# Three edits to a one-core decoder layer: matmuls of 512 columns in the second FFN's out stages, the eighth early weight slab loaded last, a_proj's merged parts made later

## The reference, cut to what matters

```python
h = modulate(x, norm_ffn1, sh1, sc1)
x = x + 0.5 * g1 * swiglu(h, w_ffn1_in, w_ffn1_out)     # (silu(h @ Wa) * (h @ Wb)) @ W_out
h = modulate(x, norm_mix, sh2, sc2); proj = h @ w_in     # z, xBC, dt, u, gates
p_a = ssd_mixer(...) @ w_a_proj                          # "a_proj"
p_b = glu_a * sigmoid(glu_g)                             # from the S5 branch
merged = sigmoid(gate_a) * p_a + sigmoid(gate_b) * p_b
x = x + g2 * (merged @ w_out)
h = modulate(x, norm_ffn2, sh3, sc3)
x = x + 0.5 * g3 * swiglu(h, w_ffn2_in, w_ffn2_out)     # D_FF = 5504
return rms_norm(x, norm_final)
# mods (sh1 ... g3) = silu(c) @ w_ada + b_ada, nine vectors of 2048
```

## Time and profile before

| | before |
|---|---|
| three timed runs | 2510.43, 2515.06, 2516.42 us, median 2515.06 |
| the profiled execution | 2511.76 us, of which its span is 2510.0 |
| PE busy | 2411.1 us, 96% of the span |
| VectorE (DVE), ScalarE (ACT) busy | 1730.3 us (69%), 1037.4 us (41%) |
| mean granted TensorE clock | 0.988 of full |
| HBM read and written | 232 GB/s over the span |

### The profile page before, as it was taken

How to read it: one execution, slowest core, us unless ns; L and a number is a source line. 1 busy time by engine, 2 the same in 40 slices (tenths; PEclk the granted TensorE clock), 3 DMA queues, 4 the chain that set the end, 5 groups by cost and what they waited for, 6 DMA issues and landing times.

```text
span 2510.0 us, 39646 instructions
## 1 busy us (share of the span) xinstructions
PE 2411.1 (96%) x16260; PEld 2187.6 (87%) x16260; DVE 1730.3 (69%) x2028; ACT 1037.4 (41%) x1111; POOL 227.8 (9%) x257
## 2 busy tenths in 40 slices
PE   6799999999999999999999999999999999999998
PEld 3488799888899999889899999999888899888998
DVE  3376877778778778888976776776877455444543
ACT  3243343443443454444345444333433444344433
POOL 1421313142223000000000000000000000000000
PEclk8999999999999999999999999999999999999999
DMA  9986877878787865555565466787678556555652
GB/s 359 382 267 242 295 263 259 292 252 308 259 279 267 305 235 169 180 175 198 177 228 167 142 212 221 254 299 250 234 273 297 168 184 202 188 192 172 197 177 97
DMA packets 296997, 584.69 MB, mean 233 GB/s; under 512 B 10324, under 2 KB 35412, under 8 KB 295316
## 3 DMA queue, kind: packets, MB, share of 16 engines
q1 hardware_dynamic: 291408, 559.98, 65.3%
q0 software_dynamic: 4144, 22.28, 2.5%
q10 hardware_dynamic: 1300, 0.35, 0.1%
HBM read 569.98 MB, written 12.58 MB: 232 GB/s over the span
## 4 chain that ended last, share of the span: by engine, by line
PE 49%; DVE 6%; ACT 1%; issue 1%; ACTq 0%; DVEq 0%
PE gps L305 45%; PE mps L305 3%; DVE wlo L914 2%; DVE t L1441 1%; DVE acc L932 1%; ACT whi L537 1%; PE mps L1721 0%; DVE tab L1484 0%; DVE wi L1478 0%; DVE E L1403 0%; DVE wi L1456 0%; DVE wr L1452 0%; DVE wr L1474 0%; DVE xw L1129 0%; DVE E L1408 0%
## 5 line engine op out<-in xcount | busy, mean ns | idle before, releaser
L914 DVE TENSOR_TENSOR wlo<-raw,whi 128x1024 fp32r<-128x1024 f32 x800 | 986.5, 1275 | 584.9 <-ACT whi L537 582.1
L537 ACT ACTIVATE whi<-raw 128x1024 fp32r<-128x1024 f32 x800 | 803.2, 1052 | 1239.3 <-PE gps L305 1204.1
L305 PE MATMUL gps<-whi,hs 128*128 128x512 f32 (+1 forms) x2816 | 875.3, 388 | 16.6 <-DVE wlo L914 11.8
L305 PEld LDWEIGHTS gps<-whi,hs 128*128 128x128 f32 x2816 | 528.9, 188 | 141.5 <-issue 22.3
L305 PE MATMUL gps<-hs,whi 128*128 128x256 f32 x3072 | 566.8, 287 | 16.8 <-DVE wlo L914 12.1
L305 PE MATMUL gps<-wlo,hs 128*128 128x512 f32 (+1 forms) x1408 | 542.9, 386 | 0.0
L305 PEld LDWEIGHTS gps<-hs,whi 128*128 128x128 f32 x3072 | 483.7, 194 | 27.3 <-DVE wlo L914 15.0
L305 PE MATMUL gps<-ffs,whi 128*128 128x256 f32 x2752 | 498.7, 284 | 5.3 <-DVE wlo L914 5.3
L305 PE MATMUL gps<-hs,wlo 128*128 128x256 f32 x1536 | 437.1, 285 | 0.0
L305 PEld LDWEIGHTS gps<-ffs,whi 128*128 128x128 f32 x2752 | 429.1, 192 | 7.2 <-DVE wlo L914 6.9
L305 PE MATMUL gps<-ffs,wlo 128*128 128x256 f32 x1376 | 389.3, 283 | 0.0
(11 more groups left out here) (270 smaller groups left out, 1412.9 us busy)
## 6 DMA issues: line engine op xcount, KB each, us to landing
raw<-in_w_ffn_in_dram SPq DMA_DIRECT2D x160, 1024.0 KB
raw<-in_w_ada_dram SPq DMA_DIRECT2D x112, 1024.0 KB
raw<-in_w_in_dram SPq DMA_DIRECT2D x80, 1024.0 KB
raw<-in_w_ffn_out_dram SPq DMA_DIRECT2D x56, 1024.0 KB
pre<-in_w_ada_dram SPq DMA_DIRECT2D x32, 1024.0 KB, 14.3
raw<-in_w_ffn_out_dram SPq DMA_DIRECT2D x40, 768.0 KB
raw<-in_w_b_glu_dram SPq DMA_DIRECT2D x32, 512.0 KB
raw<-in_w_a_proj_dram SPq DMA_DIRECT2D x16, 1024.0 KB
```

The costliest lines, as they stand in the source:

```text
L305: return pe.matmul(out, lhsT, rhs, start=start, stop=stop, skip_group_check=True)
L537: act.activation(whi[:, mpos % SPLIT, h, :], raw[:, pos % RING, h, :], ACT.Copy).then_inc(hi_ready, 1)
L914: ins = dve.tensor_tensor(wlo[:, mpos % SPLIT, h, :], raw[:, pos % RING, h, :], whi[:, mpos % SPLIT, h, :].bitcast(F32), ALU.subtract)
```

## The change

**1. Wide out stages.** In both out stages of the second FFN (`ph.wide`), the high weight block meets both parts of the activation in one matmul of 512 columns, so each product is two matmuls, of 512 and 256 columns. The sums of a tile now stand in two halves of a whole bank (`wps[:, j]`), so a group takes all four banks of `gps`. ACT copies them to SBUF: tiles 0 and 1 when they are complete, tile 2, then tile 3 (`kept`). DVE adds both halves of each kept tile to xT, 8 instructions a group. In the very last group DVE adds straight from PSUM (`add_last`).

**2. The eighth early slab.** Slab m = 7 is loaded behind chunk 7's four blocks. PE does early tiles 18 and 19 after `total(6)` instead of behind chunk 7's first two blocks, tiles 20 and 21 behind the first two, and nothing behind the last two.

**3. a_proj's merged parts.** `merged_hi` goes behind the next slab's `hi` on ACT, `merged_lo` behind the second next slab's `lo` on DVE.

```diff
+        self.wide = evac == "resid" and gate == 2
+        self.rounds = (2 if self.wide else 1) * bodies
...
-                        for m in {0: (), 6: (5, 6, 7), 7: ()}.get(q, (q - 1,)):
+                        for m in {0: (), 6: (5, 6), 7: (7,)}.get(q, (q - 1,)):
...
+                    elif ph.wide:
+                        n = 2 * i + g
+                        if r.t + n:
+                            act.wait_ge(sem("x_added"), r.t + n)
+                        act.wait_ge(sem("tiles_done"), 2 * (r.t + n) + 1)
+                        act.activation(kept[0][:, :, :], wps[:, 0:2, :], ACT.Copy).then_inc(psum_free(0), 1)
+                        act.wait_ge(sem("tiles_done"), 2 * (r.t + n) + 2)
+                        act.activation(kept[1][:, 0, :], wps[:, 2, :], ACT.Copy)
+                        act.wait_ge(slab_done, m_end)
+                        act.activation(kept[1][:, 1, :], wps[:, 3, :], ACT.Copy).then_inc(psum_free(1), 1)
...
-                    act.wait_ge(sem("merged"), n + 1)
-                    act.activation(hs[:, 4 * n:4 * n + 4, 0, :], ga[:, 4 * n:4 * n + 4, :], ACT.Copy
-                                   ).then_inc(sem("merged_hi"), 1)
+
+                    def merged_hi():
+                        act.wait_ge(sem("merged"), n + 1)
+                        act.activation(hs[:, 4 * n:4 * n + 4, 0, :], ga[:, 4 * n:4 * n + 4, :], ACT.Copy
+                                       ).then_inc(sem("merged_hi"), 1)
+
+                    later.append(merged_hi)
...
+                                if later:
+                                    later.pop()()
...
+            def add_kept(ph, n, h):
+
+                dve.wait_ge(psum_free(h), r.q + n + 1)
+                for part in range(2):
+                    for j in range(2):
+                        ins = gated_add(ph, 4 * n + 2 * h + j, kept[h][:, j, S * part:S * part + S])
+                    if part == 0:
+                        link(ins)
+                if h:
+                    ins.then_inc(sem("x_added"), 1)
+                    if ph.norm == 3:
+                        dve.wait_ge(sem("x_added"), r.t + n + 1)
+                        gains(ph, n)
+
+            def add_last(ph, m_end):
+
+                for j in range(4):
+                    if j == 0:
+                        dve.wait_ge(sem("tiles_done"), 2 * (r.t + 3) + 1)
+                    elif j == 2:
+                        dve.wait_ge(sem("tiles_done"), 2 * (r.t + 3) + 2)
+                    elif j == 3:
+                        dve.wait_ge(slab_done, m_end)
+                    link(gated_add(ph, 12 + j, wps[:, j, 0:S]))
+                    gated_add(ph, 12 + j, wps[:, j, S:2 * S]).then_inc(sem("x_new") if j < 3 else psum_free(1), 1)
...
-                    later.append(merged_lo)
+                    later.append(lambda: later.append(merged_lo))
...
+                        if q == 7:
+                            e = (20, 21, -1, -1)[t]
                         if e >= 0:
                             early_tile(e)
                     total(q)
+                    if q == 6:
+                        early_tile(18)
+                        early_tile(19)
...
+                def slab_wide(g, i, s, mp, k0):
+                    for j in range(4):
+                        if s == 0 and j % 2 == 0:
+                            pe.wait_ge(psum_free(j // 2), r.q + 2 * i + g)
+                        for k in range(ph.chunks[s]):
+                            hi = whi[:, mp % SPLIT, k, P * j:P * j + P]
+                            lo = wlo[:, mp % SPLIT, k, P * j:P * j + P]
+                            both = moving[:, k0 + k, :, :].rearrange("p w s -> p (w s)")
+                            mm(pe, wps[:, j, :], hi, both, k0 + k == 0, False)
+                            ins = mm(pe, wps[:, j, 0:S], lo, moving[:, k0 + k, 0, :], False,
+                                     k0 + k == sum(ph.chunks) - 1)
+                        yield ins
```

More of the change, by code:

```diff
@@ L221, in build @@
         gated = at("gated", T, [P, 2, COLS])
+        kept = [half, at("kept1", W, [P, 2, COLS])]
         sq = at("sq", T, [P, 4, S])
@@ L582, in first_two @@
                 for s in range(2):
+                    if s == 1 and between is not None:
+                        between()
                     if i is None:
@@ L678, in gemm @@
                     act.wait_ge(sem("bbar_ready"), 1)
+                if ph.evac == "pair" and r.t:
+                    act.wait_ge(sem("x_added"), r.t)
                 def body(i, nxt):
@@ L691, in body @@
                                 next(side, None)
+                        between = None
+                        if ph.wide:
+                            between = lambda: evacuate(ph, i, 1, m0 + i * mper + 2 * ph.slabs, 0)
                         if g == 0:
@@ L698, in body @@
                         elif nxt == "loop":
-                            first_two(ph, i, side)
+                            first_two(ph, i, side, between)
                         elif nxt is not None and ph.norm is not None:
@@ L702, in body @@
                         elif nxt is not None:
-                            first_two(nxt, side=side)
+                            first_two(nxt, side=side, between=between)
                         if g == 1:
@@ L707, in body @@
                                     pass
-                        evacuate(ph, i, g, m0 + i * mper + (g + 1) * ph.slabs, r.q + i + 1)
-                if ph.bodies > 1 and not ph.side and ph.norm is None and ph.evac != "mul_a":
+                        if not ph.wide or ph.norm is not None and 2 * i + g == 3:
+                            evacuate(ph, i, g, m0 + i * mper + (g + 1) * ph.slabs, r.q + i + 1)
+                if ph.bodies > 1 and not ph.side and ph.norm is None and ph.evac != "mul_a" and not ph.wide:
                     if after_norm:
@@ L965, in first_two @@
                     if s == 1 and between is not None:
-                        multiply(*between)
+                        between()
                     if i is None:
@@ L1091, in body @@
                                 next(side, None)
+                                if ph.wide and gg == 1 and s == 1:
+                                    add_kept(ph, 2 * i, 1)
                         if g == 1:
-                            between = (ph, m0 + i * mper + 2 * ph.slabs, r.q + i + 1) if ph.evac == "pair" else None
+                            m_end, between = m0 + i * mper + 2 * ph.slabs, None
+                            if ph.evac == "pair":
+                                between = lambda: multiply(ph, m_end, r.q + i + 1)
+                            elif ph.wide:
+                                between = lambda: add_kept(ph, 2 * i + g, 0)
                             if nxt == "loop":
@@ L1246, in early @@
             def early(ph, following):
-                first_two(following, between=(ph, 8, 1))
+                first_two(following, between=lambda: multiply(ph, 8, 1))
                 evacuate(ph, 0, 1, 8, 1)
```

68 lines of the change are left out of this document (48 added, 20 removed).

## The result

| | before | after |
|---|---|---|
| median of the timed runs on the same chip | 2515.1 us | 2496.9 us (2492.9 to 2497.5) |
| ratio to before | | 0.993, 95% interval 0.9915 to 0.9946 |
| the profiled execution | 2511.8 us, span 2510.0 | 2496.3 us, span 2494.6 |

The change takes 18 us off; the interval of the ratio leaves out 1. The forecast was 2493, the range 2482 to 2505.

The account below looks back on a forecast made before the run. PE was taken as the bound, busy 96% of the span; terms -9.2 + 0.1 + 0.8 - 4.4 - 7.5 = -20.2 us gave 2491.6 from the profiled execution or 2494.9 from the median, forecast 2493, range 2482 to 2505.

Parts of the forecast that it names:

- 1a: Wide out stages: one matmul fewer in each of 688 products saves 0.0133 us each, 9.2 us off; bounds 0 to 18.3.
- 1b: Group ends of the wide out stages: ACT's copies free the banks 0.86 us before PE wants them, cost 0.
- ACT rival: PE waits for ACT's first copy at seven group starts, 3.75 us each, 26 in all: 2519 us; chance 4%.
- 1c: Tail of the last out stage: last addition ends 1.85 us behind PE against 1.08 before, 0.8 us more.
- 2, the eighth slab: Prologue: chunk 7's first block lands at 111.4, PE starts slab 6 at 125.0 instead of 129.4, 4.4 us off; bounds 0 to 4.9.
- 3, a_proj: Gaps behind a_proj's groups 0 and 2 close, 2 x 3.75 = 7.5 us off, 5.5 at the least, 7.6 at most.
- no slack at all: a_proj: DVE's next `lo` ends at 1597.4, just when PE wants it; perhaps 0.1 to 0.3 us.

Follow-up runs that it names:

- part 2 alone: Kernel before with only the eighth slab loaded last and its early tiles moved: 2509.9 us, ratio 0.9982.
- the low part left in its place: Changed kernel, but in a_proj only the merged high part is made later, the low part as before the change: 2498.0 us, ratio 0.9937.
- the run with one at every group: Changed kernel with throwaway matmuls of 128 to 512 columns (one, or twelve at group 0) at each group's start in the wide out stages: 2498.3 us.
- the last run: Changed kernel plus last group's tile 0 told when complete, wide form in w_out, one 128-column throwaway matmul ahead of first stage's second group: 2492.1 us, ratio 0.9927.
- ACT's copies later: Changed kernel with ACT's copies of a finished group put behind the rounding of the second next slab: 2527.7 us, ratio 1.0059.
- part 1 alone: Kernel before with only the wide out stages, the two other edits undone: 2508.0 us, ratio 0.997.
- grouped by width: Changed kernel with each tile's 512-column matmuls of a slab first, then its 256-column ones, in the wide out stages: 2497.3 us, ratio 0.9938.
- the second run of the changed kernel: The changed kernel measured once more, nothing altered: 2498.0 us, ratio 0.9928.
- part 3 alone: Kernel before with only the edits to a_proj's merged_hi and merged_lo: 2507.5 us, ratio 0.997.

## Why the prediction was right, and where it was not

**1a, the fixed part: right for the second stage, half for the first.** 368 products at 0.3467 give 368 x 0.0133 = 4.9 us, as worked out (4.8 by the stage's length). The 320 of the first took 0.3533, so 320 x 0.0067 = 2.1 where 4.3 was taken. The mis-sized term is 688 x 0.0133 = 9.2; it was 7.0. The step behind it, that two widths agree on 0.0133 and so a mixed pair has the sum of both, was an inference from streams of one width, and the prediction said that no row had a mixed pair. Its bounds (0 to 18.3) held. The Trainium skill (page "TensorE: Matmul & The Clock Gate", section "Back-to-back issue gap") gives N / 2.4 + 2.5 ns for a single warm matmul, by which the pair would take an estimated 325 ns. The traces show 347 and 353, and it does not agree here either.

**1b, evacuation: right.** PE waits for none of the seven copies, with 0.79 to 0.89 us to spare where 0.86 was worked out. The ACT rival stands with its price corrected: seven gaps of 3.1 us, and a half clock behind three.

**1c, the tail: right,** 1.86 us behind PE against 1.85.

**2, the eighth slab: right in its mechanism, and 5.1 us in this execution where 4.4 was worked out and 4.9 was the bound.** Chunk 7's first block at 110.97 (111.4 forecast), the last at 118.99 (119.5), the bias at 121.86 (122.5), slab 6 at 124.55 (125.0), 5.06 us earlier than before. Each step came about half a microsecond earlier than worked out, since the first block did. The kernel with part 2 alone has 4.5 by its ratio. What the working did not see is the idle time that the new order leaves to PE at chunk 7's end, 1.6 us ahead of the last block and 0.7 ahead of the sum. In four of the eleven traces with part 2 the clock fell behind it, and 1.4 to 3 of the 5 us were lost again (last section).

**3, a_proj: right.** 3.7 us at both groups, 7.4 in all (7.5). DVE's chain ran as worked out, its `lo` ending when the slab ahead was done, but "no slack at all" left out the sum of `w_ada` products that PE makes in between; 0.75 us of slack were there. The run with the low part left in its place showed what happens when 1.1 us more stands in that chain, gaps of 0.42.

**The sum.** With what was measured for each, -7.0 + 0.8 - 4.9 - 7.4 = -18.5 us; the medians differ by 18.2. Against the sum of the prediction, -20.2, the 2.2 us of 1a are missing, and part 2 makes up 0.5. The forecast of 2493 was 3.9 too low; about 2 of this is the first stage, and the rest the base, which was set half-way between the profiled execution and the median of the timed ones, where the medians alone gave 2494.9. The profiled executions show only 15.4 us on their spans: the one of the kernel before lay 3.3 us under its median, and the one of the kernel after holds 3.3 us of delays that six others with the same code at that place don't have (below).

## What to carry to other kernels

Price an edit by the start-to-start spacing of the very sequence that it makes; where the trace has only streams of one width, keep a bound on both sides, for a mixed stream can sit at more than one pace. A gap in PE costs its idle time for sure and the half clock behind it only sometimes, so a rival's price has two ends. Start to count a stage's gain ahead of its first wait: 1.4 us in w_out were 0.3 when the wait at its entry was counted too. And when one engine's queue holds a late operation ahead of an urgent one (ACT's rounding ahead of the next slab's `hi`), the order in that one queue is worth most of the gain, here 4.9 of 7.4 us.

## What the runs showed of the hardware

**Two paces of one instruction pair.** A 512-column and a 256-column matmul in turn, at a granted clock of 1.00 and with no wait, take 0.3467 or 0.3533 us a pair. The slow pace held for up to 320 pairs in a row, the fast one for 240. One matmul of 128 columns in the middle of a stage moved it from the slow to the fast pace in three cases of three (twice in the run with one at every group, once in the last run), and one of 512 in mid-stage and twelve ahead of a stage to the slow pace; at the entry of the stage one of 128 did nothing. Breaks moved it as well: in the run with ACT's copies later, some of the gaps and of the transposes between did, either way. Which state of PE this is stays open: the runs show that it is neither the place in the program nor the width of the stream ahead by itself.

**The clock behind a gap.** Of seven gaps of the same 3.1 us, three were followed by a stretch at a granted clock of 0.50 and four by none. The gap of 2.0 us at a_proj's groups 0 and 2 had such a stretch behind it in all six cases (the kernels before, with part 1 alone and with part 2 alone). Behind the idle 1.6 and 0.7 us at chunk 7's end seven traces with part 2 stay at 1.00 and four fall. The kernel after, and the one grouped by width, whose prologue is the same:

```profile
122.00:126.00 4.00, 4.00 (x19) 3.28 (x18) 3.61 (x11) 2.75 (x6) 0.00 (x0) 1.00 1.05 385
```

```profile
122.00:126.00 4.00, 4.00 (x10) 3.18 (x11) 3.66 (x11) 1.81 (x4) 0.00 (x0) 0.50 1.05 387
```

`hi` of slab 7 starts at 124.8 to 125.6 in the seven and at 126.4 to 128.0 in the four. What tells the cases apart is open.

**Delays that no edit explains.** In the S5 stretch the kernel after falls back by 3.3 us against the kernel before, in two places. The slab whose `hi` starts at 1096.83 takes 15.97 us to the next one (14.46 before), and the two slabs from 1230.97 on take 22.28 (20.45 before). The same two delays are in the kernels with part 2 alone, with only the high part later and with ACT's copies later. Neither is in the kernel before, the second run of the changed kernel, the one with part 1 alone and five more that have all three parts; the one with part 3 alone and the last one have 1.0 us of the first. PE's waits from 860 to 1300 us in the kernel after:

```profile
PE gps L310 <- DVE wlo L952: 13.2, 8, 3.8
PE mps L310 <- DVE tab L1569: 9.3, 7, 2.9
```

The same lines say 11.7 and 9.0 in the second run of the same program. The granted clock from 1236 to 1249 us differs too: 0.74 in the kernel after, 0.87 before, 0.90 in the second run and 1.00 in the one with throwaway matmuls at each group. A difference of spans between two single executions therefore carries 3 us that no edit made, and this is why effects of this size were read here stage by stage.
